# A hybrid decoder layer in float32: norm weights multiplied into token rows instead of their transposes, and the small projection block first

## What is computed

```python
def rms_norm(x, g):
    y = x * lax.rsqrt(jnp.mean(x * x, axis=-1, keepdims=True) + EPS)
    return y * g

def hybrid_layer(x, mem, norm_mix, w_in, ...):
    u = rms_norm(x, norm_mix)
    proj = u @ w_in            # 8936 columns
    z, xbc, dt_raw, q, k, v, qi, ki, wi, g_ssm, g_att = split(proj)
    y_ssm = ssm_branch(z, xbc, dt_raw, ...) @ w_ssm_out
    y_att = dsa_branch(q, k, v, qi, ki, wi) @ w_att_out
    mix = sigmoid(g_ssm) * y_ssm + sigmoid(g_att) * y_att
    x = x + mix @ w_mix_out
    x = x + cross_attention(rms_norm(x, norm_x), rms_norm(mem, norm_mem), w_xq, w_xkv, w_xo)
    x = x + hierarchical_moe(rms_norm(x, norm_moe), ...)   # 32 experts of 3 x 2 MB
    return x
```

## Time and profile before

| | us |
|---|---|
| median of 3 runs | 1034.36 |
| lowest, highest | 1031.45, 1034.37 |
| the profiled execution | 1032.8 |
| its span, first to last instruction | 1031.1 |
| PE busy | 949.9 (92%) |
| DVE busy | 450.6 (44%) |
| ACT busy | 307.5 (30%) |
| mean granted TensorE clock | 0.968 |

### The profile page before, as it was taken

How to read it: one execution, slowest core, us unless ns; L and a number is a source line. 1 busy time by engine, 2 the same in 40 slices (tenths; PEclk the granted TensorE clock), 3 DMA queues, 4 the chain that set the end, 5 groups by cost and what they waited for, 6 DMA issues and landing times.

```text
span 1031.1 us, 14486 instructions
## 1 busy us (share of the span) xinstructions
PE 949.9 (92%) x5791; PEld 671.8 (65%) x5791; DVE 450.6 (44%) x850; ACT 307.5 (30%) x505; POOL 109.0 (11%) x120
## 2 busy tenths in 40 slices
PE   3999899999999999989889999998989899898995
PEld 3999888898998999779675344444434344443443
DVE  4578996666666765464545121212111121211113
ACT  4455446657557443354340000000000000000002
POOL 2000026845551000000000000000000000000000
PEclk8999899999999999999987999999999899998998
DMA  9455444343235755576273999999999999999991
GB/s 221 135 165 169 136 142 124 123 127 119 83 123 164 205 174 195 169 268 236 89 293 137 424 420 420 421 422 422 422 422 421 422 422 421 422 422 422 421 387 41
DMA packets 110332, 277.72 MB, mean 269 GB/s; under 512 B 14858, under 2 KB 78386, under 8 KB 85706
## 3 DMA queue, kind: packets, MB, share of 16 engines
q1 hardware_dynamic: 110138, 276.50, 71.1%
q10 hardware_dynamic: 144, 0.52, 0.1%
HBM read 275.96 MB, written 1.05 MB: 269 GB/s over the span
## 4 chain that ended last, share of the span: by engine, by line
PE 62%; DVE 12%; DMA 12%; issue 6%; POOL 4%; ACT 3%; SPq 1%; DVEq 0%; POOLq 0%; ACTq 0%
PE bank L1799 17%; DMA up_b<-in_w_e_up_dram 12%; PE bank L1442 8%; PE bank L1444 8%; PE bank L1443 8%; PE bank L1829 8%; DVE lo_w L910 4%; PE bank L1787 4%; POOL work L566 3%; PE bank L1816 2%; ACT hi_w L592 2%; DVE work L1059 2%; DVE work L1060 1%; POOL ysT L554 1%; PE bank L1720 1%
## 5 line engine op out<-in xcount | busy, mean ns | idle before, releaser
L1442 PE MATMUL bank<-u_hi,hi_w 128*128 128x256 f32 x624 | 185.0, 297 | 6.2 <-DVE lo_w L910 6.2
L1444 PE MATMUL bank<-u_hi,lo_w 128*128 128x256 f32 x624 | 178.8, 286 | 0.0
L910 DVE TENSOR_TENSOR lo_w<-raw_w,hi_w 128x2048 fp32r<-128x2048 f32 x68 | 154.8, 2281 | 54.9 <-ACT hi_w L592 54.7
L1443 PE MATMUL bank<-u_lo,hi_w 128*128 128x256 f32 x560 | 160.7, 287 | 0.0
L1799 PE MATMUL bank<-up_a,xg 128*64 128x512 f32 x256 | 122.1, 630 | 19.2 <-DMA up_b<-in_w_e_up_dram 19.2
L592 ACT ACTIVATE hi_w<-raw_w 128x2048 fp32r<-128x2048 f32 x68 | 128.4, 1889 | 32.1 <-PE bank L1444 29.1
L1442 PEld LDWEIGHTS bank<-u_hi,hi_w 128*128 128x128 f32 x624 | 122.1, 196 | 9.7 <-issue 8.9
L1829 PE MATMUL bank<-down_a,moe_buf 128*64 128x512 f32 x256 | 115.0, 601 | 9.5 <-DVE xg L1378 7.6
L1799 PE MATMUL bank<-up_b,xg 128*64 128x512 f32 x256 | 122.3, 631 | 0.0
L1444 PEld LDWEIGHTS bank<-u_hi,lo_w 128*128 128x128 f32 x624 | 121.8, 195 | 0.0
L869 ACT ACTIVATE y_pair_hi<-bank 128x512 fp32r<-128x512 f32 x32 | 17.4, 595 | 338.8 <-PE bank L1829 338.8
(11 more groups left out here) (317 smaller groups left out, 1786.8 us busy)
## 6 DMA issues: line engine op xcount, KB each, us to landing
raw_w<-in_w_in_dram SPq DMA_DIRECT2D x34, 1024.0 KB, 5.5
up_b<-in_w_e_up_dram SPq DMA_DIRECT2D x32, 1024.0 KB, 23.2
up_a<-in_w_e_up_dram SPq DMA_DIRECT2D x32, 1024.0 KB, 21.1
down_a<-in_w_e_down_dram SPq DMA_DIRECT2D x32, 1024.0 KB, 17.4
down_b<-in_w_e_down_dram SPq DMA_DIRECT2D x32, 1024.0 KB, 19.5
gate_a<-in_w_e_gate_dram SPq DMA_DIRECT2D x16, 1024.0 KB, 19.2
gate_b<-in_w_e_gate_dram SPq DMA_DIRECT2D x16, 1024.0 KB, 21.2
gate_c<-in_w_e_gate_dram SPq DMA_DIRECT2D x16, 1024.0 KB, 20.5
```

The source lines that it names most:

```text
L910: tt(lo_w[:, m % RING, 0:w], raw_w[:, m % RING, 0:w], hi_w[:, m % HI_RING, 0:w].bitcast(F32), ALU.subtract).then_inc(lo_done, 1)
L1442: mm(dst, left[0], right[0], start=first, stop=False)
L1443: mm(dst, left[0], right[1], start=False, stop=False)
L1444: return mm(dst, left[1], right[0], start=False, stop=last)
```

## The change

Three things change together.

- The weights of norm_mix, norm_mem and norm_x are no longer 8 numbers on each partition, multiplied into the transposes, but a row of 1024 sent to all 128 partitions (`gain_row`, 512 KB for each of the three transfers). DVE multiplies it in the instruction that scales the token rows.
- The multiply into `tr_tmp` goes. ACT and DVE take the high and the low part from PSUM, and PE may fill a bank again only after DVE has read the low part (`tr_evac`, no longer `tr_gain`).
- `tm` and its steps come ahead of `kk`, k and ki. DVE makes the low part of unit 0 before the low parts of the transposes.

```diff
-        steps = (["k", "ki", "tm0", "tm1"] + [f"qi{b}" for b in range(4)] + [f"bc{b}" for b in range(8)]
+        steps = (["tm0", "tm1", "k", "ki"] + [f"qi{b}" for b in range(4)] + [f"bc{b}" for b in range(8)]
...
-        units, LAST_STEP = [("kk", None, KT), ("tm", None, KT)], {"kk": "ki", "tm": "tm1"}
+        units, LAST_STEP = [("tm", None, KT), ("kk", None, KT)], {"kk": "ki", "tm": "tm1"}
...
-            sp.dma_start(g_mix, norm_mix[0, :].rearrange("(p t) -> p t", t=KT)).then_inc(gmix_in, 16)
+            sp.dma_start(gain_row, norm_mix[0:1, :].to_broadcast([P, D])).then_inc(gain_in, 16)
...
+                    sp.wait_ge(xn_ready, 2)
+                    sp.dma_start(gain_row, norm_mem[0:1, :].to_broadcast([P, D])).then_inc(gain_in, 16)
...
+                if name == "mo00":
+                    sp.wait_ge(xn_ready, 4)
+                    sp.dma_start(gain_row, norm_x[0:1, :].to_broadcast([P, D])).then_inc(gain_in, 16)
...
-                        act.wait_ge(tr_gain, g + 1)
+                        act.wait_ge(tr_ready, g + 1)
                         nc.scalar.activation(dst[:, 4 * q:4 * q + 4, P * i:P * i + P],
-                                             tr_tmp[:, g % 2, :].rearrange("p (k t) -> p k t", k=4), ACT.Copy)\
+                                             bank[2 + g % 2][:, :].rearrange("p (k t) -> p k t", k=4), ACT.Copy)\
                             .then_inc(tr_hi, 1)
...
+                dve.wait_ge(gain_in, 16 * n + 16)
                 for i in range(NT):
-                    ts_(dst[:, i, :], src[:, i, :], st[:, c + 2 + i:c + 3 + i], None, ALU.mult).then_inc(xn_ready, 1)
+                    stt(dst[:, i, :], src[:, i, :], st[:, c + 2 + i:c + 3 + i], gain_row, ALU.mult, ALU.mult)\
+                        .then_inc(xn_ready, 1)
+
+            def columns_of(i, hiT, loT, tiles=1):
+
                 for ii in range(i, i + tiles):
                     for q in range(2):
                         g = group[0]
-                        dve.wait_ge(tr_ready, g + 1)
-                        if g >= 2:
-                            dve.wait_ge(tr_evac, g - 1)
-                        ps = bank[2 + g % 2][:, :].rearrange("p (k t) -> p k t", k=4)
-                        gb = gain[:, 4 * q:4 * q + 4].unsqueeze(2).to_broadcast([P, 4, P])
-                        tt(tr_tmp[:, g % 2, :].rearrange("p (k t) -> p k t", k=4), ps, gb, ALU.mult)\
-                            .then_inc(tr_gain, 1)
...
+                        dve.wait_ge(tr_hi, g + 1)
+                        blk = (slice(None), slice(4 * q, 4 * q + 4), slice(P * ii, P * ii + P))
+                        tt(loT[blk], bank[2 + g % 2][:, :].rearrange("p (k t) -> p k t", k=4), hiT[blk].bitcast(F32),
+                           ALU.subtract).then_inc(tr_evac, 1)
                         group[0] += 1
...
-            columns_of(0, g_mix, u_hi, u_lo, NT)
+            split_lo_through(0)
+            dve.wait_ge(xn_ready, NT)
+            columns_of(0, u_hi, u_lo, NT)
...
-                        pe.wait_ge(tr_gain if split else tr_evac, g - 1)
+                        pe.wait_ge(tr_evac, g - 1)
...
-            w = use_unit("kk")
-            fm_step("k", w, 0, u_parts)
-            fm_step("ki", w, P, u_parts)
             w = use_unit("tm")
...
+            w = use_unit("kk")
+            fm_step("k", w, 0, u_parts)
+            fm_step("ki", w, P, u_parts)
```

More of the change, by code:

```diff
@@ L49 @@
 HI_RING = 3
-N_PRM = 13
+N_PRM = 11
 MOE_SLOTS = 8
@@ L158, in hybrid_block @@
         pXT = flat_work[:, 2048:3072].rearrange("p (n w) -> p n w", n=2)
-        tr_tmp = flat_work[:, 3584:4608].rearrange("p (n w) -> p n w", n=2)
+        gain_row = flat_work[:, 3584:4608]
         mix_tmp = flat_work[:, 512:1024].rearrange("p (n w) -> p n w", n=2)
@@ L165, in hybrid_block @@
         sgain = prm[:, 120:136]
-        g_mix, g_mem, g_x, g_moe = (prm[:, 136 + 8 * i:144 + 8 * i] for i in range(4))
+        g_moe = prm[:, 136:144]
         dskip = prm[:, 168:184]
@@ L207, in hybrid_block @@
         x_in = sem("x_in")
-        gmix_in = sem("gmix_in")
+        gain_in = sem("gain_in")
         ident_ready = sem("ident_ready")
-        tr_gain = sem("tr_gain")
         tr_hi = sem("tr_hi")
@@ L658, in _ @@
             act.wait_ge(consts, 1)
+            for i in range(NT):
+                n = STEP[f"tm{i}"]
+                evac(f"tm{i}", small_tm[:, i, :], src=bank[n % 2][:, 0:TM_W])
             for name, d in (("k", kz), ("ki", kiz)):
@@ L664, in _ @@
                 nc.scalar.activation(d[64:128, 1, :], bank[n % 2][64:128, 0:SEQ], ACT.Copy).then_inc(evac_act, 1)
-            for i in range(NT):
-                n = STEP[f"tm{i}"]
-                evac(f"tm{i}", small_tm[:, i, :], src=bank[n % 2][:, 0:TM_W])
             act.wait_ge(prm_in, 16 * N_PRM)
@@ L925, in norm_rows @@
                 dve.wait_ge(rstd_done, n + 1)
+                dve.wait_ge(gain_in, 16 * n + 16)
                 for i in range(NT):
-                    ts_(dst[:, i, :], src[:, i, :], st[:, c + 2 + i:c + 3 + i], None, ALU.mult).then_inc(xn_ready, 1)
-            def columns_of(i, gain, hiT, loT, tiles=1):
-                def low(i, q, g):
-                    dve.wait_ge(tr_hi, g + 1)
-                    blk = (slice(None), slice(4 * q, 4 * q + 4), slice(P * i, P * i + P))
-                    tt(loT[blk], tr_tmp[:, g % 2, :].rearrange("p (k t) -> p k t", k=4), hiT[blk].bitcast(F32),
-                       ALU.subtract).then_inc(tr_evac, 1)
-                before = None
+                    stt(dst[:, i, :], src[:, i, :], st[:, c + 2 + i:c + 3 + i], gain_row, ALU.mult, ALU.mult)\
+                        .then_inc(xn_ready, 1)
+            def columns_of(i, hiT, loT, tiles=1):
                 for ii in range(i, i + tiles):
@@ L941, in columns_of @@
                         g = group[0]
-                        dve.wait_ge(tr_ready, g + 1)
-                        if g >= 2:
-                            dve.wait_ge(tr_evac, g - 1)
-                        ps = bank[2 + g % 2][:, :].rearrange("p (k t) -> p k t", k=4)
-                        gb = gain[:, 4 * q:4 * q + 4].unsqueeze(2).to_broadcast([P, 4, P])
-                        tt(tr_tmp[:, g % 2, :].rearrange("p (k t) -> p k t", k=4), ps, gb, ALU.mult)\
-                            .then_inc(tr_gain, 1)
-                        if before is not None:
-                            low(*before)
-                        before = (ii, q, g)
+                        dve.wait_ge(tr_hi, g + 1)
+                        blk = (slice(None), slice(4 * q, 4 * q + 4), slice(P * ii, P * ii + P))
+                        tt(loT[blk], bank[2 + g % 2][:, :].rearrange("p (k t) -> p k t", k=4), hiT[blk].bitcast(F32),
+                           ALU.subtract).then_inc(tr_evac, 1)
                         group[0] += 1
-                low(*before)
             def columns_f32(i, gain, dstT):
@@ L1197, in _ @@
                 if b == 5:
-                    columns_of(0, g_mem, u_hi, m_lo)
+                    columns_of(0, u_hi, m_lo)
                 if b == 7:
-                    columns_of(1, g_mem, u_hi, m_lo)
+                    columns_of(1, u_hi, m_lo)
             dve.wait_ge(gn_rstd, 1)
@@ L1236, in residual_and_norm @@
                             dve.wait_ge(rstd_done, 2 * nn - 1 + i)
-                            ts_(dst[:, i, :], xres[:, i, :], r, None, ALU.mult).then_inc(xn_ready, 1)
+                            if prefix == "mo":
+                                dve.wait_ge(gain_in, 48)
+                                stt(dst[:, i, :], xres[:, i, :], r, gain_row, ALU.mult, ALU.mult).then_inc(xn_ready, 1)
+                            else:
+                                ts_(dst[:, i, :], xres[:, i, :], r, None, ALU.mult).then_inc(xn_ready, 1)
             for j in range(4):
@@ L1243, in _ @@
             split_lo_through(UN["vx10"])
-            columns_of(0, g_x, a_hi, a_lo, NT)
+            columns_of(0, a_hi, a_lo, NT)
             split_lo_through(UN["qx0"])
@@ L1446, in _, with transposes_of @@
             u_parts, m_parts, a_parts, y_parts = (u_hi, u_lo), (u_hi, m_lo), (a_hi, a_lo), (y_hi, y_lo)
-            def transposes_of(xn, i, split=True):
+            def transposes_of(xn, i):
                 pe.wait_ge(xn_ready, group[0] // 2 + 1)
@@ L1752, in _ @@
             for i in range(NT):
-                transposes_of(xn2, i, split=False)
+                transposes_of(xn2, i)
                 pe.wait_ge(tr_evac, 14 + 2 * i)
```

7 lines of the change are left out of this document (2 added, 5 removed).

## The result

| | before | after |
|---|---|---|
| median, us (12 runs of each) | 1032.80 | 1035.58 |
| lowest to highest | 1031.45 to 1034.37 | 1033.45 to 1037.11 |
| the profiled execution | 1032.8 | 1034.09 |
| its span | 1031.1 | 1032.4 |

The ratio after to before is 1.0023 (95% interval 1.0013 to 1.0033): 2.4 us slower (2.8 by the medians). The same kernel, measured a second time in another series, came to 1.0022 (1.0012 to 1.0032).

The account below looks back on a forecast made before the run. The experts' weight stream bounds the end, so edits on PE's chain ahead of it count one to one. Opening +2.2 - 0.1, memory +1.1, cross-attention +0.9 make +4.1 us; forecast 1037.0 us, range 1030.5 to 1040.5.

Parts of the forecast that it names:

- The case that I held likeliest: Whole kernel: low clock through tm and added waits make it slower, +4.1 us, 1037.0 us; chance 0.48.
- PE's start of tm: Opening: PE starts tm at 16.4 us instead of 19.6, -3.2 us.
- The clock under tm: Opening: tm's 48 narrow matmuls run at 1.2 GHz, 0.227 us each, 10.9 us in all.
- The rise in k: Opening: clock rises some 4.3 us into k and ki, which take 7.7 us and end at 35.0, +2.2 us.
- qi1 bound by DVE: Step sizes: DVE's chain stays as long and PE waits for qi1's low part; counted -0.1 us.
- Memory rows: 331 to 342 us: row norm +0.47 and second tile's waits for low parts +0.65, together +1.1 us.
- Ahead of the cross-attention: 439 to 458 us: row norm +0.45 and waits for low parts net +0.45, together +0.9 us.
- Nothing behind: Experts' stream: it shifts by the sum, so the shift at the first gate slots equals that at the end.
- The first rival: Opening: the clock rises during tm, after 20 matmuls; -1.1 us in all, 1031.7 us; chance 0.20.
- The second: Opening: the clock is high when tm starts and stays; -3.7 us in all, 1029.1 us; chance 0.07.
- The third: Memory and cross-attention rows: added waits cost nothing, only the opening's +2.1 us remains, 1034.9 us; chance 0.18.
- The fourth: Opening: tm or the gain row lands late, up to 2 us more, 1039 us; chance 0.07.

Follow-up runs that it names:

- wide_tm: The changed kernel with tm's 48 matmuls made 256 columns wide instead of 104; 1033.39 us, ratio 0.9997 to the kernel before.
- after: The changed kernel itself, as first measured and profiled; 1035.58 us, ratio 1.0023 to the kernel before.
- after_again: The changed kernel unaltered, measured once more in another series; 1034.72 us, ratio 1.0022 to the kernel before.
- after_held: The changed kernel with unread matmuls in two idle PE stretches, near 332 and 441 us; 1034.69 us, ratio 1.0024 to the kernel before.
- late_old_held: The changed kernel with old norms at memory and cross-attention rows, plus unread matmuls in two idle PE stretches there; 1033.25 us, ratio 1.0002 to the kernel before.
- late_norms_old: The changed kernel with the norm part undone at the memory rows and ahead of the cross-attention queries; 1035.66 us, ratio 1.0023 to the kernel before.
- early_steps: The changed kernel with small parameter transposes and step-size exponentials moved ahead of k and ki; 1033.79 us, ratio 1.0016 to the kernel before.
- four_banks: The changed kernel with four PSUM banks instead of two for the first three norms' transposes; 1031.55 us, ratio 0.9987 to the kernel before.
- warm_up: The changed kernel with unread matmuls ahead of and between the opening's transposes and ahead of tm; 1032.57 us, ratio 0.9989 to the kernel before.
- combined: The changed kernel with old later norms, four banks for the opening's transposes, early step-size chain, unread matmuls in the opening; 1030.48 us, ratio 0.9981 to the kernel before.
- old_norm_tm_first: The kernel before with only the order changed, tm ahead of kk; 1034.69 us, ratio 1.0022 to the kernel before.

## Why the prediction was right, step by step, and where it was off

The case that I held likeliest came: slower by a little, through the low clock under tm and three small costs. The median, 1035.58, is 1.4 below the 1037.0 forecast; the runs before had a median of 1032.8, not the 1034.36 of the first three, and the effect itself is +2.4 by the ratio (1.3 to 3.4 by its interval) where the sum of my terms is +4.1. The mechanism was right, the size 1.7 times too large, and a range from 1030.5 to 1040.5 would have held a gain of 2 us too.

Over the five executions of the changed opening the three places cost 1.34, 1.23 and 0.53, together 3.1. The 0.7 between this and the ratio isn't explained; of the kernel before there is one profiled execution only, so its own opening and routing aren't averaged.

- **PE's start of tm.** 16.4 forecast, 15.95 to 16.45 in five executions of the changed opening. Row norms 1.28 against my 1.22. tm's weights reached ACT at 9.85, not 10.4. Right.
- **The clock under tm.** Low through all of tm, as taken from the 36-column matmuls of the earlier trace rows; wide_tm shows that the width is the cause. tm took 10.45 us, not 10.9: 0.218 for each matmul, not 0.227. The mechanism is right; the 0.45 us, from a price taken from 36-column matmuls, is the largest part of what the opening was overrated by.
- **The rise in k.** I took one value, 4.3 us into k, from the one execution that I had. Five executions (after, after_again, after_held, late_old_held, late_norms_old) give 3.0, 4.0, 4.9, 3.4 and 4.3 (the clock's first record less the end of tm), 3.9 on the mean, and k with ki took 7.6 on the mean where I had 7.7. So the value was near, but it differs by nearly 2 us between executions. ki was done at 33.64, 34.31, 34.97, 33.91 and 34.57, on the mean 34.28, and I had 35.0: of the 0.72, 0.45 are tm's matmuls, 0.20 its earlier start and the rest k and ki. The shift of the opening is 0.69, 1.37, 2.03, 0.98 and 1.64, on the mean 1.34 where I forecast 2.1.
- **qi1 bound by DVE.** Right: PE idled 1.1 us for it, DVE's wait for the small transposes stands in the trace, and in early_steps PE's idle is gone.
- **Memory rows.** +1.1 forecast, 1.23 measured (0.53 the row norm, 0.70 the banks); four_banks, with the banks' wait gone, has 0.50 there, and late_norms_old, with both gone, 0.08. Right.
- **Ahead of the cross-attention.** +0.9 forecast, 0.53 measured. The row norm is right; the further 0.45 was an error of mine. I compared an end that held the row norm's shift already (458.3) with the 457.86 of before, and then added the row norm again. The wait for low parts is there (1.10 us at 453.89, where 0.43 was), and most of what it costs, 0.67, comes back where PE had waited for vx11: two matmuls that were 0.79 apart there (0.41 of it idle) are 0.23 apart.
- **Nothing behind.** The shift at the first gate slots should have been the whole, and it is the difference at the end: 1.31 and 1.3 in the profiled pair. It is 1.1 short of the 2.45 at 485 us, by the clock in the routing of the one execution before. Two single traces can't show a 2 us effect at their ends.

The first rival, a rise in the middle of tm, is out for this kernel and comes true for wider matmuls. The second, a clock held from the start, came true as its condition said, with no idle time ahead of tm: the shift at 52 us is -3.00 in warm_up and -3.68 in combined, where the clock held for tm alone and other edits have their part. The case against it, that the clock was low at the transposes, left out that it rises behind them, in the kernel before at 13.7. The third, added waits at no cost, is refuted by late_old_held against after_held. The fourth is out, since tm and the gain row came in time; for kk first it would have been true. The plain reading of the rule I had weighed (the Trainium skill, "TensorE: Matmul & The Clock Gate", section "What's actually happening") would have misled here: PE's busy share was 100% for 10 us, and the clock didn't rise.

## What to carry to other kernels

Where the clock is low, try the wide matmuls first, and bring the narrow ones to PE while the clock is high: the same 48 narrow matmuls cost 5.5 us or 10.4 us here by what stood ahead of them. That an idle stretch ahead of them is what loses the clock rests on four single executions (none and 0.87 us: held; 1.32 and 1.46: fell) and isn't shown apart from them. Where a consumer is made to release a buffer later (here the low part in place of the multiply), count the wait at each place, and give the buffer a second pair first. And when undoing one part to price it, look in the trace for falls of the clock at PE's idle stretches: late_norms_old saved 1.8 us in its parts and lost 1.6 to one fall, and its median showed no gain.

## What the runs showed of the hardware that I hadn't expected

- The clock rose behind sixteen float32 transposes of 128 columns in a row: it stood at 1.00 from 14.6 us on in four_banks, from 13.7 in the kernel before. Behind eight, a pause of 0.8 us and eight more it was low when tm began, in the kernel after.
- The granted clock could fall in the middle of matmuls without a gap: at 18.0 and 16.5 us, 2.4 and 1.8 us into tm, behind idle stretches of 1.46 and 1.32 us. Behind 0.87 us in combined it held through tm.
- A SCALAR_TENSOR_TENSOR with two float32 tensors of 1024 elements takes 1.28 us, a TENSOR_SCALAR of the same size 0.75.
- A fall at PE's idle stretch near 441 cost 1.6 us (late_norms_old, old_norm_tm_first, combined), 1.5 (wide_tm, the growth of 2.00 less the row norm's 0.53) and once 2.8 (after_again, 3.35 less 0.53). In four_banks, the sixth with a fall there, the shift grew by 0.74 in all, with PE's waits for the banks gone in the same place.
